# Two places moved from the v rows to the u rows of a gather buffer

## The reference, cut to what matters

```python
u_sel = jnp.take(u, expert, axis=0)
v_sel = jnp.take(v, expert, axis=0)
act = jax.nn.gelu(jnp.einsum('btd,bthkd->bthk', hx, u_sel), approximate=False)
return jnp.einsum('bthk,bthkd->btd', (gate * act).astype(h.dtype), v_sel)
```

## Time and profile before

| | us |
|---|---|
| median of three runs | 2037.94 |
| lowest and highest | 2035.21, 2042.11 |
| the profiled execution, its own time | 2036.36 |
| its span in the trace | 2034.6 |
| mean granted TensorE clock | 0.982 |
| PE busy | 1774.8 (87%) |
| DVE busy | 1356.7 (67%) |
| ACT busy | 854.1 (42%) |
| POOL busy | 1037.5 (51%) |

### The profile page before, as it was taken

The page is one execution under the profiler, slowest core; times in us unless marked ns, Lnnn a source line. Parts: engine busy times, 40 slices in busy tenths (PEclk is TensorE's granted clock), DMA queues, the critical chain, the costliest instruction groups (busy, mean ns, idle before and its releaser), DMA issues.

```text
span 2034.6 us, 21815 instructions
## 1 busy us (share of the span) xinstructions
PE 1774.8 (87%) x6507; PEld 1006.1 (49%) x6507; DVE 1356.7 (67%) x2955; ACT 854.1 (42%) x2034; POOL 1037.5 (51%) x1064
## 2 busy tenths in 40 slices
PE   8999777779988897797898977977777999999998
PEld 6655222213344452243545424422222897778997
DVE  4577988556478569846975994454554367578874
ACT  3444434330157133313742444343433455655663
POOL 0767777765567657755775676667775000000000
PEclk9999999999999899998998998999999999999999
DMA  7999999999999999999999999999999554455664
GB/s 282 388 407 408 409 409 409 409 402 388 378 406 383 408 409 409 409 409 400 379 403 409 409 409 409 409 409 406 409 409 388 180 180 139 130 161 175 187 188 136
DMA packets 194308, 704.27 MB, mean 346 GB/s; under 512 B 21624, under 2 KB 23040, under 8 KB 193936
## 3 DMA queue, kind: packets, MB, share of 16 engines
q0 software_dynamic: 152064, 553.72, 68.9%
q1 hardware_dynamic: 40672, 147.44, 21.0%
q10 hardware_dynamic: 1456, 1.72, 0.2%
HBM read 701.60 MB, written 1.06 MB: 345 GB/s over the span
## 4 chain that ended last, share of the span: by engine, by line
PE 41%; DMA 31%; POOL 10%; DVE 8%; issue 6%; ACT 3%; SPq 0%; DVEq 0%; ACTq 0%; POOLq 0%
DMA a<-in_peer_v,eidx 17%; PE ps L967 17%; DMA a<-in_peer_u,eidx 13%; PE ps L678 11%; POOL a L507 5%; POOL a L519 5%; PE ps L584 5%; DVE a L2022 3%; PE ps L701 3%; PE ps L830 2%; DVE ring_r L2209 1%; PE ps L713 1%; PE ps L637 0%; ACT a_r L1608 0%; DVE a L2163 0%
## 5 line engine op out<-in xcount | busy, mean ns | idle before, releaser
L678 PE MATMUL ps<-a,diag 128*128 128x512 f32 (+1 forms) x1880 | 906.1, 614 | 210.5 <-DMA a<-in_peer_v,eidx 165.3
L2022 DVE SCALAR_TENSOR_TENSOR a<-a,ps 128x1024 f32<-128x1024 f32 x528 | 641.3, 1219 | 397.0 <-DMA a<-in_peer_u,eidx 373.2
L678 PEld LDWEIGHTS ps<-a,diag 128*128 128x128 f32 (+1 forms) x1880 | 329.5, 189 | 734.6 <-issue 647.7
L507 POOL DMA_INDIRECT a<-in_peer_u,eidx x528 | 518.0, 981 | 317.2 <-DVE a L2022 155.1
L519 POOL DMA_INDIRECT a<-in_peer_v,eidx x528 | 518.6, 982 | 211.5 <-issue 132.7
L1348 ACT ACTIVATE gel<-dots 128x1 f32<-128x1 f32 x528 | 104.3, 201 | 697.2 <-DVE a L2022 692.0
L967 PE MATMUL ps<-a_r 128*128 128x256 f32 (+1 forms) x1096 | 258.9, 327 | 0.4 <-DVE a_r L2268 0.4
L967 PEld LDWEIGHTS ps<-a_r 128*128 128x128 f32 x1096 | 181.9, 188 | 21.7 <-issue 2.8
L2209 DVE TENSOR_TENSOR ring_r<-wring,a_r 128x1024 fp32r<-128x1024 f32 x95 | 116.0, 1223 | 82.0 <-ACT a_r L1608 81.6
L1360 ACT ACTIVATE diag<-cstc,cga 128x128 f32<-128x128 f32 (+1 forms) x398 | 158.3, 398 | 13.1
L967 PE MATMUL ps<-a_r,ring_r 128*128 128x256 f32 x512 | 142.5, 278 | 0.0
(11 more groups left out here) (301 smaller groups left out, 1783.7 us busy)
## 6 DMA issues: line engine op xcount, KB each, us to landing
wring<-in_units SPq DMA_DIRECT2D x246, 512.0 KB, 4.5
a<-in_peer_u,eidx POOLq DMA_INDIRECT x528, 13.0
a<-in_peer_v,eidx POOLq DMA_INDIRECT x528, 13.1
late<-in_units SPq DMA_DIRECT2D x8, 512.0 KB, 15.6
a<-in_units SPq DMA_DIRECT2D x7, 512.0 KB, 14.7
a<-in_poolm SPq DMA_DIRECT2D x1, 1632.0 KB, 8.5
late<-in_cs SPq DMA_DIRECT2D x1, 1280.0 KB, 8.0
h<-in_xin SPq DMA_DIRECT2D x2, 512.0 KB, 4.3
```

Of the source, the lines that this page charges most:

```text
L507: g.indirect_dma_start(ug[:, n % NU, :], None, peer_u, bass.IndirectOffsetOnAxis(ap=eidx[:, t, k:k + 1], axis=0))\
L678: last = nc.tensor.matmul(ps[0:P, b + j, :], diag[:, pe_slots[n] % ND, 0:P], vg[:, k % NV, j * 512:(j + 1) * 512], start=False, stop=n == ...
L2022: v.scalar_tensor_tensor(ug[:, n % NU, :], ug[:, n % NU, :], 1.0, ps2(0) if t == 2 else ps2(4), ALU.mult, ALU.mult, accum_out=dots[:, k % ...
```

## The change

`NU` becomes 8 and `NV` 6: eight places for u rows and six for v rows, in place of six and eight. `a1` keeps its width; the v places start at column 8192 of it in place of 6144. `sums_slot` now indexes the v places by the slot's number in the whole program (n) in place of its number in its tile (k). With eight places the two were the same, since each tile's first slot is a multiple of 16; with six they are not. Every other use of the places goes by n already.

```diff
-NU = 6
-NV = 8
+NU = 8
+NV = 6
@@ sums_slot
-                pe.wait_ge(S(f"v{k % NV}"), vfill)
+                pe.wait_ge(S(f"v{n % NV}"), vfill)
                 for j in range(2):
                     last = nc.tensor.matmul(ps[0:P, b + j, :], diag[:, pe_slots[n] % ND, 0:P],
-                                            vg[:, k % NV, j * 512:(j + 1) * 512], start=False,
+                                            vg[:, n % NV, j * 512:(j + 1) * 512], start=False,
                                             stop=n == 16 + 4 * SLOTS - 1)
```

## The result

| | before | changed |
|---|---|---|
| median us (4 runs each) | 2039.11 | 2057.22 |
| lowest and highest | 2035.21, 2042.11 | 2056.77, 2058.0 |
| the profiled execution, its own time | 2036.36 | 2058.0 |
| its span | 2034.6 | 2056.2 |

A forecast was written before the change was run, and what follows sets the result against it. The prediction took the DMA engines as the bound before 1582 us where their rate is full, and PE after. Losses of 3.0 + 3.5 + 2.5 = 9.0 us gave a median of 2047.0 us, range 2033 to 2057.

The forecast's parts named there:

- much slower: Rival: late u rows hold up DVE in both stick-breaking stretches, then sums come later; 2056 us, chance 0.13 (2053 and more).
- What bounds the kernel: DMA engines bound full stretches before 1582 us, PE the tail; time changes only where the rate isn't or stops being full.
- C: 1120 to 1160 us: less work queued before POOL's pause, so the DMA queue runs dry; 2.5 us, bounds 0 and 5.1.
- The places u and v, and POOL's order: Whole gather phase: in-order launches tie u rows to v rows; waits for dots all but vanish and bring nothing.
- B: 950 to 1050 us: v rows wait for later sums, POOL can't catch up; 3.5 us, bounds -4.0 and 4.6 plus 3.
- The two late launches: V rows at 958.82 and 1015.95 us, forecast to launch 3.2 and 4.6 us late, waiting for PE's sums.
- A: 560 to 650 us: POOL runs less far ahead and a v row launches late; 3.0 us, bounds 0 and 5.1.
- The launch of 603.04: V row at 603.04 us, forecast to launch 3.1 us late, with no POOL slack and an empty DMA queue.
- the page that was weighed: Skill page implying 3.2 us per gather against the trace's 6.1 with an empty queue; the prediction stayed with the trace.
- Same: Rival: launches come late but rows arrive in time, POOL catching up in DVE's pauses; 2040 us, chance 0.28 (2034 to 2043).
- Faster: Rival: waits for dots vanish where the rate isn't full and v places free in time; 2030 us, chance 0.12.

The follow-up runs named there:

- u6v6: The changed kernel with its two extra u places taken away, six u and six v: 2165.9 us, ratio 1.0041 to the kernel before of its set.
- the second trace: Trace of the kernel before, rerun without a change: traced execution 2041.55 us; the runs' median is 2040.23 us, ratio 1.0001.
- six_b: The kernel before with an added wait making v rows of slots 296 to 345 wait as with six places: 2160.8 us, ratio 1.0001.

## Why the prediction was right, and what it missed

The forecast was a median of 2047.0 us, a loss of 9.0; measured are 2057.22 and 18.1, twice as much. The direction, the mechanism and the places held, the sum did not. The median stands at the very end of the range (2033 to 2057), which reached that far for the chance given to *much slower* and not by the forecast's own terms, so that this was luck. Of the three terms, 3.0, 3.5 and 2.5 us, the dots show some 6.5, 9.4 to 10.0 and 0.7 to 1.4.

**What bounds the kernel.** Held. Full stretches and tail kept their time (408 GB/s; the tail's 440.42 us of PE work in 452), and all of the loss shows in, or right behind, the stretches where the rate was below 409, and a little in C. The list of such stretches lacked one, 450 to 500 us.

**The places u and v, and POOL's order.** Held. The waits changed over as written (sums past 200 us, dots below 40: 248.2 and 15.1), and by u6v6, on the slower chip, the u places brought nothing that can be measured. The rates fell as written too: 380 to 364 GB/s from 600 to 650, and 372 (359 in the second trace) to 349 from 960 to 1010. The last gather was to be launched some 9 us later; it came 25.7 us after that of the first trace of before and 19.9 after that of the second.

**B.** Right row by row, wrong in the sum. The two late launches were worked out as 3.2 and 4.6 us and came as 3.3 and 4.8. The step that failed is "I take 3.5, between the two rows": it treats as two readings of one loss what are two losses one after the other. After the first, POOL launches without pause up to 1010 us, as the prediction itself said, so that nothing is made up before the second comes. Their sum, 7.8 us, was to be taken; between slots 318 and 350 the dots fall back by 10.0 us against the one trace of before and 9.4 against the other. The bound above, 7.6 us, was too low as well. For the last us or two of this step (10.0 and 9.4 against 7.8) the traces were not followed further, and their cause is open.

**A.** The sign was right and the place wrong. The launch of 603.04 came 3.3 us late, for 3.1 (by its own rows 3.2), and cost nothing there that the dots show. What cost was priced at nothing: while PE is the bound POOL can run ahead by two slots less, and DVE came to the end of this shorter store at 583 to 596 us: 5.5 us of waits for u rows before the first head. The prediction counted those 5.1 us of missing DMA work, but left them out of the sum since "from 560 to 600 the rate is full". It is full (410 GB/s in both), and just for that reason what is missing at 560 can't be fetched by 596. Much of it goes missing before 500 us already: at 409 GB/s the fall from 395 or 378 to 340 from 450 to 500 is 6.7 or 4.6 us of DMA work, that from 373 or 367 to 363 from 500 to 560 is 1.5 or 0.6. At slot 318 the loss is 5.5 us against the second trace of before and 11.4 against the first, of which 2.3 lay ahead of slot 183 already; the forecast had 3.0 and an upper bound of 5.1. The step itself, 6.5 us, is the same against both; those 2.3 us need not be the change, since the second trace of before is 3.4 us late there, and the same holds for the 2.5 us between slots 206 and 256.

**C.** Right in kind: the queue, 8.0 us at its shortest, runs empty at 4.9. It cost 0.7 to 1.4 us against the 2.5 taken, within its bounds; seven and seven places lose 1.3 us there too. The trace also bears on the page that was weighed. With an empty queue the medians of the landing times are 6.1 to 6.9 us in the three traces of the first kind of chip, and the shortest single row took 4.0. The Trainium skill, page "DMA: Bandwidth & Descriptors", section "Anatomy of one DMA — SWDGE (gpsimd) path", would have 3.2 us for such a gather, an estimate by its fixed part and rate; no row here is that short, so the measurement decides.

**The rivals.** The forecast's three places are the ones, but the time is that of the rival *much slower* (2056), and its first half is what the traces show: late u rows hold up DVE, on the way into the one stretch and inside the other. It was given 0.13 because its price was put as "pays twice" without a row for it; the row was there, as the second late launch of B. *Same* is out, since the last gather came far more than 2 us late. *Faster* is out: its tell, a v row at B's place no later than 959 us, came at 973.68, or 962.2 with what was late before taken off (worked out: 962.0).

**Open.** That A and B carry the loss on the first chip is read from traces alone: the experiments that put six places into single stretches ran on the other kind of chip, where no loss could be told in these stretches and the whole change cost 0.58%. That late u rows are the path is read from the waits in the traces; the run with three slots between u and v fits it and was on the slower kind too. Nor was a kernel with three slots and the places of before tried, or the kernel before traced on the slower kind.

## What to carry to other kernels

Where one in-order queue feeds two buffers, count which buffer's place comes free last at each launch that is late, and add up the late launches that have no slack between them; don't average them. A buffer's place is worth what the queue's depth lacks at the entry into the next stretch, so price the store that a slow stretch lets build up as part of the stretch behind it. When the waits on two buffers add up to the same total for several splits, moving places gains nothing, and here it cost 0.25 to 0.28% all the same. The order of the launches is the next thing to try: one slot more between u and v took the changed kernel back to the level of before, within the noise.

## What the runs showed of the hardware

Two kinds of chip, for one program: medians of 2038 to 2040 us with a mean granted clock of 0.98, and of 2142 to 2157 us with 0.94 to 0.95. From 1160 to 1560 us the kernels traced on the first kind move 407 to 409 GB/s, those traced on the other 381 to 396. Changes may be ordered differently on them: six v places in slots 296 to 345 cost nothing that can be told on the one (six_b), where on the other the changed kernel falls back by 9 to 10 us in slots 318 to 350.

On one kind of chip, two executions of the same kernel differ by 5.8 us at the last dot. Part of it goes with the granted clock from 450 to 500 us, 0.94 in the first trace of before and 0.85 in the second, with PE busy almost throughout from 470 us on in both; this is the second trace:

```profile
450.00:500.00 50.00, 44.17 (x97) 15.65 (x96) 36.59 (x67) 7.28 (x23) 28.76 (x31) 0.85 0.99 378
```

3.4 us of the 5.8 are there by slot 183, 2.5 more come between 206 and 256. A loss of a few us in one stretch is not to be read from one pair of traces.
